# The order of token tiles and weight chunks at the end of five weight products in a two-block transformer kernel

## The chip, the core and the metric

The kernel runs on one core of a Trainium2 chip. The metric is the device time of one execution, in microseconds (us); shorter is better. The kernel before takes 2402.28 us, the median of three runs.

## What is computed

A sequence of 512 tokens of width 1024 passes two blocks in fp32. What matters here are the places where a product with a weight matrix ends a sublayer and a normalisation follows:

```
# first block, twice (MLA layer, then sliding-window layer)
y = attention(x)                       # ends in  o @ w_o          (1024 x 1024)
x = layernorm(alpha * x + y)
x = layernorm(alpha * x + relu(x @ w_up)**2 @ w_down)   # w_down: 4096 x 1024
# second block
y = (gm*(hm @ w_mlstm_out) + gd*(hd @ w_diff_out) + gr*(hr @ w_ret_out)) @ w_out
x = x + rmsnorm(y) ; h2 = rmsnorm(x)
x = x + rmsnorm((silu(a) * u) @ w_ffn_out)
```

## The kernel before

**Products.** Every fp32 factor is split into a high part and a remainder, and a product is three matmuls (high by high, high by remainder, remainder by high; `mm3`, line 590), all written at line 588. Weights come in chunks of 128 x 2048 numbers. Chunk c goes through slot c mod 2: SP loads it into `RAW` (`load`, line 429), ACT copies it to the high part `WH` in two halves (`split`, line 1438), DVE subtracts to get the remainder `WL` in two halves (`split`, line 2102) and then raises `lo_ready`, on which PE waits before it uses the chunk. Since there are two slots, ACT may not write `WH` of chunk c before PE has finished chunk c-2; PE says that with `chunk_done`:

```
if c >= 2:
    act.wait_ge(chunk_done, c - 1 + i * per)                          # line 1447
for part in (slice(0, n // 2), slice(n // 2, n)):
    nc.scalar.activation(WH[s][:, part], RAW[s][:, part], ACT.Copy).then_inc(hi_ready, 1)
```

**A projection by tokens.** The 512 tokens are four tiles of 128, with a PSUM bank `A[t]` each. An output half of 512 columns needs two chunks (kh = 0 and 1), each with four of the eight 128-row pieces of the contraction. So a (tile, chunk) pair is a block of 4 x 3 = 12 matmuls of 512 columns. `tokens` (line 596) takes all four tiles through one chunk, then through the next.

**The last two chunks.** `tokens_edge` (line 627) handles the second output half. It runs over eight blocks in an order written out by hand, waits for the second chunk's `lo_ready` at the first block that uses it, and, ahead of its last block, puts the transposes of the normalised tiles 0 and 1 (`edge_turn`, line 647). `features_edge` (line 659) follows with the first product of the next sublayer, and takes the transposes of tiles 2 and 3 in its middle. `tokens_edge` is called five times: after `w_o` of the MLA layer (line 939, called ln0 below), after the first MLP's `w_down` (line 992, ln1), after `w_o` of the window layer (line 1127, ln2), after the second MLP's `w_down` (line 992, pre), and after `w_out` (line 1395, post). The final `w_ffn_out` product has an order of its own (line 1418) that is not touched. If the first chunk of such an edge is called e, the second is e+1, and it shares its slot with e-1, the last chunk of the first output half.

**Beside it.** While PE takes the first output half, DVE adds the residual and takes half moments of each tile (`residual`, line 466, h = 0; `mlp`, lines 2528 to 2543; `product_out`, line 2865, with ACT's `product_squares`, line 2009, at post), and its `split` of chunk e+1 stands behind the fourth tile of that work. In the second half DVE and ACT normalise each tile as it is finished (`norm_edge`, lines 2448 and 1626; lines 1752 to 1768 for pre; lines 2875 to 2892 and 2028 to 2041 for post). ACT's `split` of the next sublayer's first chunk stands behind the normalisation of tiles 0 and 1 and waits for chunk e to be done, which is when tile 3's block of chunk e ends. POOL only loads vectors here; SP's next load waits for `lo_ready` of e+1.

Of the kernel before, what the change touches and what calls it, by code (L numbers as in the profile page):

```python
# [139 lines left out]
def build(nc, a, out):  # L140
# [53 lines left out]
    def grid(t, k, n, at=0):  # L194
        return t[:, at:at + k * n].rearrange("p (k n) -> p k n", k=k)
# [4 lines left out]
    def tok(t):  # L200
        return slice(t * P, (t + 1) * P)
# [63 lines left out]
    def slot(c):  # L265
        return c % 2
# [319 lines left out]
    def _(pe):  # L586
# [3 lines left out]
        def mm3(dst, lh, ll, rh, rl, first, last):  # L590

            mm(dst, lh, rh, first, False)
            mm(dst, lh, rl, False, False)
            return mm(dst, ll, rh, False, last)
# [32 lines left out]
        def tokens_edge(c, rnd, xh, xl, name, done):  # L627

            pe.wait_ge(lo_ready, c + 1)
            for t, kh in ((0, 0), (1, 0), (0, 1), (1, 1), (2, 0), (3, 0), (2, 1), (3, 1)):  # L630
                wh, wl = grid(WH[slot(c + kh)], 4, 512), grid(WL[slot(c + kh)], 4, 512)
                if kh == 0:
                    pe.wait_ge(a_free[t], rnd)
                elif t == 0:
                    pe.wait_ge(lo_ready, c + 2)
                elif t == 3:
                    for x in range(2):
                        edge_turn(name, x, done)
                for j in range(4):
                    k = 4 * kh + j  # L640
                    m = mm3(A[t][:], xh[:, k, tok(t)], xl[:, k, tok(t)], wh[:, j, :], wl[:, j, :], k == 0, k == KD - 1)
                if t == 3:
                    m.then_inc(chunk_done, 1)
                elif kh:
                    m.then_inc(tok_done, 1)

        def edge_turn(name, t, done):

            half = t // 2
            pe.wait_ge(*done(t))  # L650
            for k in range(KD):
                bank, free, n = edge_bank(name, half, k // 2)
                if t % 2 == 0 and k % 2 == 0:
                    pe.wait_ge(free, n)
                r = nc.tensor.transpose(bank[:, 256 * (k % 2) + P * (t % 2):256 * (k % 2) + P * (t % 2) + P], Y[:, t, tok(k)], ident[:])  # L655
                if t % 2 and k % 2:
                    r.then_inc(turned, 1)
# [279 lines left out]

        tokens(BASE["wo0"][0] + 1, slot(BASE["wo0"][0] + 1), XH, XL, 4, 4, 512, BASE["wo0"][1])
        tokens_edge(BASE["wo0"][0] + 2, BASE["wo0"][1] + 1, XH, XL, "ln0", normed("ln0"))

        def seven(g, name, i):
# [28 lines left out]
        def mlp(name, first, first_done, last, last_done):  # L970

            c0, ra, rb, _, _, _ = BASE[name]
            c3 = c0 + 33

            def down(i, h):
                for kh in range(2):
                    j = 4 + 2 * h + kh
                    pe.wait_ge(mlp_lo, plain_tile(name, 0) + 4 * kh + 4)
                    tokens(c3 + j, slot(c3 + j), YH, YL, 4 * kh, 4, 512, ra + h, kh == 0, kh == 1)

            def up(i, js):
                for j in js:
                    features(c0 + 11 * i + j, slot(c0 + 11 * i + j), XH, XL, rb // 2 + 4 * i + j)

            features_edge(c0, rb // 2, first, first_done)
            for i in range(3):
                up(i, range(0 if i else 1, 4))
                seven((0 if name == "mlp0" else 3) + i, name, i)
            up(3, range(4))
            pe.wait_ge(common_done, SUMMED.index(name) + 1)  # L990
            down(3, 0)
            tokens_edge(c3 + 6, ra + 1, YH, YL, last, last_done)
# [129 lines left out]
        for k in (6, 7):  # L1122
            for t in range(T):
                r = output_products(A[t], t, (k,), False, k == 7)
                if k == 7:
                    r.then_inc(chunk_done if t == T - 1 else tok_done, 1)
        tokens_edge(BASE["wo1"][0] + 2, BASE["wo1"][1] + 1, YH, YL, "ln2", normed("ln2"))
        pre_done = lambda t: (s_("pre_n"), t + 1)
        mlp("mlp1", "ln2", normed("ln2"), "pre", pre_done)
# [1977 lines left out]
```

## Time and profile before

| | |
|---|---|
| median of three runs | 2402.28 us (2401.63 to 2402.39) |
| the profiled execution, its own time | 2400.7 us |
| its span, first to last instruction | 2398.9 us |
| PE busy | 2372.0 us (99%) |
| DVE busy | 1381.7 us (58%) |
| ACT busy | 963.4 us (40%) |
| granted TensorE clock, mean | 1.000 |

PE is TensorE; DVE, ACT, POOL and SP are VectorE, ScalarE, GpSimd and SyncE. A matmul's row shows 0.39 us although the next one starts 0.23 us after it: matmuls overlap, so starts are to be compared, not durations. "idle before" in square brackets is the idle time of the engine before an instruction, with the one that ended it.

### The profile page before, as it was taken

How to read it: one execution, taken by the hardware profiler on the slowest of the kernel's cores; microseconds unless marked ns; L12 is line 12 of the kernel's file. 1: busy time of each engine (PE TensorE's matmuls, PEld its weight loads, DVE VectorE, ACT ScalarE, POOL GpSimd, SP SyncE). 2: the span in 40 equal slices, each digit the busy share in tenths (PEclk: the TensorE clock that was granted, in tenths of full speed). 3: DMA queues.
4: the chain of work that ended last, by engine and by line, in shares of the span. 5: the costliest groups of instructions: out<-in, count | busy, mean ns of one | idle time of the engine just before them, and what ended most of it. 6: DMA issues, size and time to landing. Idle time of an engine off the chain costs nothing.

```text
span 2398.9 us, 29398 instructions
## 1 busy us (share of the span) xinstructions
PE 2372.0 (99%) x11532; PEld 1960.0 (82%) x11532; DVE 1381.7 (58%) x2079; ACT 963.4 (40%) x1720; POOL 72.7 (3%) x146
## 2 busy tenths in 40 slices
PE   8999999999999999999999999999999999999998
PEld 8778888888888888878888888888877888888887
DVE  4667877766668787675544222323356535565655
ACT  4434443335545344344444323323245534433333
POOL 3000000000000000000000000100000000000000
PEclk9999999999999999999999999999999999999999
DMA  4123324333113332322222332222321122323231
GB/s 142 53 74 128 125 81 141 106 106 102 57 54 98 114 104 74 121 88 88 80 78 71 105 105 71 85 73 88 110 64 52 61 89 82 112 70 123 88 123 70
DMA packets 177061, 219.19 MB, mean 91 GB/s; under 512 B 9987, under 2 KB 131040, under 8 KB 176816
## 3 DMA queue, kind: packets, MB, share of 16 engines
q1 hardware_dynamic: 173152, 204.82, 26.5%
q0 software_dynamic: 3792, 12.75, 1.7%
q8 instruction: 81, 1.33, 0.2%
q14 instruction: 36, 0.29, 0.0%
HBM read 215.43 MB, written 5.27 MB: 92 GB/s over the span
## 4 chain that ended last, share of the span: by engine, by line
PE 95%; DVE 3%; ACT 1%; issue 1%; DMA 0%; SPq 0%; DVEq 0%; ACTq 0%
PE B L588 44%; PE A L588 41%; PE C L588 7%; PE C L1045 1%; DVE ar L2318 0%; PE C L1316 0%; DVE WL L2110 0%; DMA X<-in_x 0%; PE C L1154 0%; PE C L655 0%; PE C L874 0%; DVE st L2420 0%; DVE XL L2265 0%; DVE Y L2439 0%; DVE X L2908 0%
## 5 line engine op out<-in xcount | busy, mean ns | idle before, releaser
L2110 DVE TENSOR_TENSOR WL<-RAW,WH 128x1024 fp32r<-128x1024 f32 (+3 forms) x346 | 395.6, 1185 | 383.1 <-ACT WH L1450 382.8
L588 PE MATMUL B<-XH,WH 128*128 128x512 f32 (+1 forms) x1432 | 542.6, 383 | 1.4 <-ACT XH L1507 0.8
L588 PE MATMUL B<-XH,WL 128*128 128x512 f32 (+1 forms) x1432 | 534.9, 377 | 0.0
L588 PE MATMUL B<-XL,WH 128*128 128x512 f32 (+1 forms) x1432 | 519.7, 378 | 2.5 <-DVE XL L2265 2.3
L1450 ACT ACTIVATE WH<-RAW 128x1024 fp32r<-128x1024 f32 (+4 forms) x362 | 353.0, 1026 | 406.9 <-PE A L588 267.1
L588 PEld LDWEIGHTS B<-XH,WH 128*128 128x128 f32 x1432 | 269.2, 188 | 68.1 <-issue 14.1
L588 PEld LDWEIGHTS B<-XH,WL 128*128 128x128 f32 x1432 | 269.2, 188 | 50.5
L588 PEld LDWEIGHTS B<-XL,WH 128*128 128x128 f32 x1432 | 259.7, 188 | 52.1 <-DVE XL L2265 4.1
L588 PE MATMUL A<-WH,XH 128*128 128x512 f32 (+2 forms) x688 | 260.6, 379 | 1.0 <-issue 1.0
L588 PE MATMUL A<-WH,XL 128*128 128x512 f32 (+2 forms) x688 | 259.2, 377 | 0.0
L588 PE MATMUL A<-WL,XH 128*128 128x512 f32 (+2 forms) x688 | 259.1, 377 | 0.0
L588 PE MATMUL A<-WH,YH 128*128 128x512 f32 x608 | 237.7, 391 | 0.2 <-DVE WL L2110 0.2
L588 PE MATMUL A<-WH,YL 128*128 128x512 f32 x608 | 236.8, 389 | 0.0
L588 PE MATMUL A<-WL,YH 128*128 128x512 f32 x608 | 236.7, 389 | 0.0
L588 PEld LDWEIGHTS A<-WH,XH 128*128 128x128 f32 x688 | 129.5, 188 | 25.2 <-issue 2.2
L588 PEld LDWEIGHTS A<-WH,XL 128*128 128x128 f32 x688 | 129.4, 188 | 23.2
L588 PEld LDWEIGHTS A<-WL,XH 128*128 128x128 f32 x688 | 129.5, 188 | 22.8
L588 PEld LDWEIGHTS A<-WH,YH 128*128 128x128 f32 x608 | 114.1, 188 | 24.9 <-DVE WL L2110 0.7
L588 PEld LDWEIGHTS A<-WH,YL 128*128 128x128 f32 x608 | 114.1, 188 | 24.0
L588 PEld LDWEIGHTS A<-WL,YH 128*128 128x128 f32 x608 | 114.2, 188 | 23.1
L588 PE MATMUL A<-ar 64*128 64x256 f32 (+7 forms) x512 | 113.0, 439 | 1.8 <-ACT ar L1839 1.8
L1453 ACT ACTIVATE YH<-ar 128x512 fp32r<-128x512 f32 (+1 forms) x86 | 51.6, 627 | 134.2 <-DVE ar L2129 81.4
(369 smaller groups left out, 2988.9 us busy)
## 6 DMA issues: line engine op xcount, KB each, us to landing
RAW<-in_w_in SPq DMA_DIRECT2D x33, 1024.0 KB, 5.1
RAW<-in_mlp_w_up SPq DMA_DIRECT2D x32, 1024.0 KB, 5.3
RAW<-in_mlp_w_down SPq DMA_DIRECT2D x26, 1024.0 KB, 5.2
RAW<-in_w_in SPq DMA_DIRECT2D x48, 512.0 KB, 4.5
RAW<-in_w_ffn_in SPq DMA_DIRECT2D x22, 1024.0 KB, 5.0
RAW<-in_w_ffn_out SPq DMA_DIRECT2D x8, 1024.0 KB, 5.0
ar<-in_mlp_w_down SPq DMA_DIRECT2D x6, 1024.0 KB, 7.6
RAW<-in_mla_w_o SPq DMA_DIRECT2D x4, 1024.0 KB, 5.0
```

What stands on the lines that cost most here:

```text
L588: return nc.tensor.matmul(dst, l, r, start=first, stop=last)
L1045: r = nc.tensor.transpose(C[kb][:, tok(x)], W_S[:, z, h, blk * P:blk * P + P], ident[:])
L1450: nc.scalar.activation(WH[s][:, part], RAW[s][:, part], ACT.Copy).then_inc(hi_ready, 1)
L1453: return nc.scalar.activation(dst, src, ACT.Copy, scale=scale)
L2110: x = tt(WL[s][:, part], RAW[s][:, part], f32(WH[s][:, part]), ALU.subtract)
```

## The change

One line: the order of the first four blocks in `tokens_edge`. Block (t, kh) is tile t with chunk kh.

```diff
         def tokens_edge(c, rnd, xh, xl, name, done):
 
             pe.wait_ge(lo_ready, c + 1)
-            for t, kh in ((0, 0), (1, 0), (0, 1), (1, 1), (2, 0), (3, 0), (2, 1), (3, 1)):
+            for t, kh in ((0, 0), (0, 1), (1, 0), (1, 1), (2, 0), (3, 0), (2, 1), (3, 1)):
                 wh, wl = grid(WH[slot(c + kh)], 4, 512), grid(WL[slot(c + kh)], 4, 512)
                 if kh == 0:
                     pe.wait_ge(a_free[t], rnd)
                 elif t == 0:
                     pe.wait_ge(lo_ready, c + 2)
```

Tile 0 gets both chunks ahead of tile 1. The matmuls, their number and their operands stay. The wait for the second chunk's `lo_ready` stays with block (0, 1) and so stands after one block of the edge in place of two. Tiles 2 and 3 keep their order.

## Rows read from the trace of the kernel before

**Rows 1.** The page: busy us (share of the span) and count of instructions by engine.
```profile
PE 2372.0 (99%) x11532; PEld 1960.0 (82%) x11532; DVE 1381.7 (58%) x2079; ACT 963.4 (40%) x1720; POOL 72.7 (3%) x146
```

**Rows 2.** PE's waits: line, releaser, us in total, times, longest us.
```profile
PE B L588 <- DVE XL L2265: 2.3, 4, 1.7
PE C L655 <- ACT Y L1453: 1.9, 2, 1.3
...
PE A L588 <- DVE WL L2110: 0.2, 1, 0.2
```

**Rows 3.** Timeline of edge ln0: start us, us, engine, line, what.
```profile
187.29 0.39 PE L588 MATMUL A<-WH,XH 128*128 128x512 f32 x1
...
187.55 2.01 ACT L1450 ACTIVATE WH<-RAW 128x1024 fp32r<-128x1024 f32 x2 [9.92 <-PE A L588]
...
188.83 2.34 DVE L2110 TENSOR_TENSOR WL<-RAW,WH 128x1024 fp32r<-128x1024 f32 x2
...
206.34 0.60 PE L655 MATMUL C<-ident,Y 128*128 128x128 f32 x4
```

**Rows 4.** Timeline of edge ln2, around PE's wait for the second chunk.
```profile
702.25 0.67 DVE L2478 TENSOR_TENSOR Y<-X,A 128x512 f32<-128x512 f32 x1
...
702.75 0.39 PE L588 MATMUL A<-WH,YH 128*128 128x512 f32 x1
...
706.19 2.34 DVE L2110 TENSOR_TENSOR WL<-RAW,WH 128x1024 fp32r<-128x1024 f32 x2
...
707.97 0.39 PE L588 MATMUL A<-WH,YL 128*128 128x512 f32 x1
708.59 0.50 PE L588 MATMUL A<-WH,YH 128*128 128x512 f32 x1 [0.23 <-DVE WL L2110]
...
709.15 0.39 PE L588 MATMUL A<-WH,YL 128*128 128x512 f32 x1
```

**Rows 5.** Timeline of edge ln1: first matmul and DVE's split.
```profile
526.43 0.39 PE L588 MATMUL A<-WH,YH 128*128 128x512 f32 x1
...
527.97 2.34 DVE L2110 TENSOR_TENSOR WL<-RAW,WH 128x1024 fp32r<-128x1024 f32 x2
```

**Rows 6.** Timeline of edge pre: first matmul and DVE's split.
```profile
1042.77 0.39 PE L588 MATMUL A<-WH,YH 128*128 128x512 f32 x1
...
1044.31 2.35 DVE L2110 TENSOR_TENSOR WL<-RAW,WH 128x1024 fp32r<-128x1024 f32 x2
```

**Rows 7.** Timeline of edge post: first matmul and DVE's split.
```profile
2015.64 0.39 PE L588 MATMUL A<-WH,XH 128*128 128x512 f32 x1
...
2017.51 2.36 DVE L2110 TENSOR_TENSOR WL<-RAW,WH 128x1024 fp32r<-128x1024 f32 x2 [0.20 <-ACT WH L1450]
```

**Rows 8.** Timeline of edge ln0: the normalised tile 1, and the next chunk's split.
```profile
201.95 1.15 ACT L1453 ACTIVATE Y<-Y,st 128x1024 f32<-128x1024 f32 x1 [1.23 <-DVE st L2441]
203.87 2.01 ACT L1450 ACTIVATE WH<-RAW 128x1024 fp32r<-128x1024 f32 x2 [0.77 <-PE A L588]
```

**Rows 9.** Timeline of edge pre: ACT and PE ahead of tile 1's transposes.
```profile
1059.35 2.01 ACT L1450 ACTIVATE WH<-RAW 128x1024 fp32r<-128x1024 f32 x2 [0.75 <-PE A L588]
...
1064.16 0.66 PE L655 MATMUL C<-ident,Y 128*128 128x128 f32 x4 [1.30 <-ACT Y L1453]
```

**Rows 10.** Timeline of edge post: ACT's chain after tile 1, and PE's wait on it.
```profile
2027.44 0.29 ACT L2020 ACTIVATE st<-st 128x1 f32<-128x1 f32 x1
2027.84 1.06 ACT L1738 ACTIVATE Y<-X 128x1024 f32<-128x1024 f32 x1
...
2046.51 0.66 PE L655 MATMUL C<-ident,Y 128*128 128x128 f32 x4 [0.57 <-ACT Y L1453]
```

**Rows 11.** Windows: us; busy PE, PEld, DVE, ACT, POOL; granted clock; DMA share, GB/s.
```profile
1072.00:1076.00 4.00, 2.51 (x19) 2.29 (x20) 3.80 (x10) 3.48 (x6) 0.00 (x0) 1.00 0.00 0
```

**Rows 12.** Timeline of PE at the kernel's start, transposes after a long idle stretch.
```profile
4.93 1.09 PE L729 MATMUL A<-ident,X 128*128 128x128 f32 x4 [4.93 <-DMA X<-in_x]
...
12.04 1.06 PE L729 MATMUL A<-ident,X 128*128 128x128 f32 x4
```

## The prediction

> **What bounds the kernel now.** I read the page first: PE is busy for 2372.0 us, 99% of the span of 2398.9 [rows 1]. So a microsecond in which PE stands still is a microsecond of the kernel, unless a later wait of PE shrinks by as much; and work of DVE or ACT is worth something only where PE waits for it. The second view is therefore PE's list of waits [rows 2]: what a faster normalisation could give back at the five edges is small, 1.9 us in two waits for a normalised tile ahead of its transposes and 2.3 us in four waits for remainders. One line of that list is on the very spot of the change: once, for 0.2 us, PE waited for a weight remainder (WL) in front of a token product. The third view is the timeline of each of the five edges, for two questions: when does the second chunk become ready, and when does PE ask for it, before and after.
>
> **The step of PE.** In edge ln0 the first matmul starts at 187.29 and the first transpose, behind seven blocks or 84 matmuls, at 206.34 [rows 3]: 19.05 / 84 = 0.227 us for a matmul, 2.72 us for a block of 12. In the order of before, PE asks for the second chunk two blocks (5.44 us) after the edge's start. The change makes it ask after one block, at 2.72 us.
>
> **When the second chunk is ready.** It shares its slot with the chunk that PE finishes at the edge's start, so ACT cannot begin its copy earlier: it begins at 187.55, 0.26 us after the edge's first matmul, and needs 2.01 us for both halves; DVE's subtraction stands behind its work on tile 3's first half and runs from 188.83 for 2.34 us, to 191.17 [rows 3]. That is 3.88 us after the edge's start: earlier than 5.44, later than 2.72. Nothing of this moves with the change, as all of it stands ahead of the first moved instruction. So a wait that was hidden behind the second block comes into the open.
>
> **What a wait costs.** Edge ln2 has this wait already [rows 4]: DVE's remainder ends at 706.19 + 2.34 = 708.53 and PE's matmul starts at 708.59, 0.06 later. The third matmul from there starts at 709.15, where an unbroken stream would have had it at 707.97 + 3 x 0.227 = 708.65, so the stream slipped by 0.50 us, of which 708.59 - 708.20 = 0.39 is waiting and 0.10 to 0.11 is slow restart. (The 0.23 in brackets is less because the previous matmul's own row lasts 0.39.) So I take for each edge: slip = end of WL + 0.06 + 0.10 - (edge start + 2.72).
>
> - ln0 [rows 3]: 191.17 + 0.16 - 190.01 = 1.32 us.
> - ln1 [rows 5]: WL ends 530.31; 530.47 - 529.15 = 1.32 us.
> - ln2 [rows 4]: WL ends 708.53; 708.69 - 705.47 = 3.22, less the 0.50 that it costs already: 2.72 us, just one block. Here the first half's product comes from a special order, all four tiles end close together, and DVE has their four residuals and half moments queued ahead of its subtraction (the second residual, at 702.25, is shown).
> - pre [rows 6]: WL ends 1046.66; 1046.82 - 1045.49 = 1.33 us.
> - post [rows 7]: WL ends 2019.87; 2020.03 - 2018.36 = 1.67 us. ACT squares tile 3 before its copy, which makes this later than the others.
>
> Sum of the slips: 1.32 + 1.32 + 2.72 + 1.33 + 1.67 = 8.36 us.
>
> **What is queued behind the wait.** On PE everything: tile 1's first block had covered it. Tile 0 is nevertheless finished earlier, by 2.72 less the gross slip (1.4 us in ln0, ln1 and pre, 1.05 in post, nothing in ln2, where it ends when it did); tile 1 and all after it are later by the full slip. The wait for tile 1's free bank costs nothing: even in ln2, where DVE is latest, it frees that bank at 702.25 + 0.67 = 702.92 [rows 4], and PE now asks for it after 708.59. SP's next load waits for `lo_ready` of the same chunk, which does not move; POOL waits only for normalised tiles and has nothing urgent.
>
> **Does the earlier tile 0 give something back?** What PE needs from it is the normalised tiles 0 and 1 in front of block (3, 1). In ln0 tile 1 is ready at 201.95 + 1.15 = 203.10 and PE comes to its transposes at 206.34 [rows 3, 8]: 3.2 us of slack, and both ends get later together. What follows on ACT and DVE hangs on the end of block (3, 0), for which ACT's next copy waits at 203.87 [rows 8]; that moves with PE. ln1 and ln2 look the same. Gain: nothing. In pre PE does wait, 1.30 us ahead of tile 1's transposes, but the chain behind it starts at ACT's copy of the next chunk at 1059.35, which waited 0.75 us for PE's block (3, 0); the squares, root and scaling of tile 1 stand behind that copy in ACT's order, and the scaling is what released PE at 1064.16 [rows 9]. This chain moves with PE, so the 1.30 stays, and so does the longest wait for remainders (1.7 us of rows 2), whose DVE chain starts from the same copy. Gain: 0, bounded by the 1.30. In post ACT has no such anchor: from the arrival of tile 1 it runs nearly unbroken to the wait of 0.57 at 2046.51. There the earlier tile 0 takes away a small gap: the root of tile 1 starts at 2027.44 and lasts 0.29, and the squares of tile 0, which wait for DVE's sum, start at 2027.84 [rows 10]. The gap is 0.11 by the rows' ends and 0.40 by their starts; ACT's rows overlap a little, so I take 0.20. Gain 0.20, bounded by the wait of 0.57. Together: 8.36 - 0.20 = 8.2 us.
>
> **The clock.** The new stall in ln2 is about 3.1 us of no matmul starts (705.47 to 708.59), the longest in the body of the kernel; the longest of before there is the 1.7 of rows 2, and the window that holds it shows a granted clock of 1.00, the 2.4 GHz level [rows 11]. So no row shows what 3 us do. The only longer idle is at the kernel's start: after 4.93 us without one, four transposes' rows last 1.09 us, and 1.06 still at 12.04 [rows 12], against 0.60 for four of the same shape in an edge [rows 3]. So that stretch ran at about half speed, for 12.04 + 1.06 - 4.93 = 8.2 us. A stretch at half speed costs half its length, so the price here is between 0 and 4.1 us. I take 0, since the stall is nearer to the 1.7 us one, which left the clock alone, and is a single one with dense matmuls on both sides. The Trainium skill, TensorE: Matmul & The Clock Gate, Part 1, says that an idle array falls to 1.2 GHz and gets 2.4 GHz back only after sustained work; that is the case just priced. The same page (Loop structure matters more than you think) would finish one output tile over the whole contraction before the next, which is what the change does for tile 0; its reason is a warm clock, and here the clock is at 1.00 either way [rows 11], so by that rule the sum gets no gain.
>
> **Rivals.**
> - *Half clock behind ln2's stall.* As above; a gain in nothing, a further cost of up to 4.1 us, around 1.6 if the stretch is as long as the stall: 2412.0 us, at most 2414.5. For it: 3.1 us is nearer to 4.93 than any stall before in the body. Against: the body's rows at 1.00. Chance 0.10.
> - *The slips are partly given back.* The waits of pre and post (1.30, 1.7, 0.57) shrink because DVE and ACT had 1 to 3 us more for tile 0: 8.4 - 3.6 = 4.8 us, 2407.1 us, at the border of no change. For it: these engines set the waits. Against: in pre the chain is anchored at PE's own block (3, 0). Chance 0.06.
> - *Faster: tile 0 first shortens the path to the transposes.* The place is the wait ahead of tile 1's transposes and the remainders behind it. If the second chunk were ready when PE asks, there would be no slips, and up to 1.9 + 2.3 = 4.2 us of waits [rows 2] would go: 2398.1 us. It decides where WL ends before edge start + 2.72 us; it ends 3.88, 3.88, 5.78, 3.89 and 4.23 us after the start in the five edges, later in all. Chance 0.02.
>
> **How the numbers follow.** The forecast (all five slips, nearly nothing back) has 0.82. The sum is made against the profiled execution, 2400.7 us with a span of 2398.9, so 2408.9; the median of the runs is 1.6 above that execution, and the same 8.2 us on 2402.28 give 2410.4. Range: below, both bounds of giveback (1.3 and 0.4 more) and the 1.6 between executions: 2407.1; above, the half clock at most of its bound, 2414.0. Some 0.2%, 4.8 us, is what a measurement of this kernel can tell from no change; 8.2 is 0.34%. Slower by more takes the forecast, the clock rival and a part of the second: 0.93; within it 0.05; faster 0.02.
>
> **What the profile after would show.** PE waiting for WL five times in place of once, with bracketed idle of about 1.05, 1.05, 2.95, 1.05 and 1.4 us (each slip less 0.10 and less the 0.16 by which a matmul's row overhangs), 7.5 in total; WL's end unmoved against the edge's start; first transposes of ln0 at 207.66, and the edges' slips adding up to 1.3, 2.6, 5.4, 6.7, 8.2; the wait of 1.30 in pre still there and the one of 0.57 in post near 0.3; the granted clock at 1.00 behind 708 + 3. I am wrong if WL ends earlier in an edge, if the pre wait shrinks, or if matmuls behind ln2's stall start 0.43 us apart.

## The result

The changed kernel takes 2410.22 us (median of seven executions, 2408.99 to 2411.35) beside 2402.24 us for the kernel before (seven, 2400.67 to 2402.64): 8.0 us more, ratio 1.0037 with a 95% interval of 1.0028 to 1.0046. It is slower, by about what the five waits add up to. The profiled execution took 2408.99 us, its span is 2407.2.

The profile after is best opened at PE's waits (line, releaser, us in total, times, longest us):

```profile
PE A L588 <- DVE WL L2110: 7.5, 5, 3.0
PE A L729 <- DMA X<-in_x: 6.5, 2, 5.1
PE B L588 <- DVE XL L2265: 2.3, 4, 1.7
...
PE C L655 <- ACT Y L1453: 1.6, 2, 1.3
```

One line has moved to the top: the wait for the second chunk's remainder was 0.2 us, once [rows 2], and is 7.5 us in five. The two kinds of wait that an earlier tile 0 might have shortened are at 2.3 and 1.6 us, where they were 2.3 and 1.9.

The five places, and with each the first transpose of that edge, from the timeline (start us, us, engine, line, what):

```profile
186.03 0.39 PE L588 MATMUL A<-WH,XH 128*128 128x512 f32 x1
187.56 2.34 DVE L2110 TENSOR_TENSOR WL<-RAW,WH 128x1024 fp32r<-128x1024 f32 x2
189.96 0.50 PE L588 MATMUL A<-WH,XH 128*128 128x512 f32 x1 [1.05 <-DVE WL L2110]
206.41 0.60 PE L655 MATMUL C<-ident,Y 128*128 128x128 f32 x4
...
526.85 0.39 PE L588 MATMUL A<-WH,YH 128*128 128x512 f32 x1
530.77 0.50 PE L588 MATMUL A<-WH,YH 128*128 128x512 f32 x1 [1.05 <-DVE WL L2110]
547.23 0.60 PE L655 MATMUL C<-ident,Y 128*128 128x128 f32 x4
...
704.40 0.39 PE L588 MATMUL A<-WH,YH 128*128 128x512 f32 x1
707.84 2.34 DVE L2110 TENSOR_TENSOR WL<-RAW,WH 128x1024 fp32r<-128x1024 f32 x2
710.23 0.50 PE L588 MATMUL A<-WH,YH 128*128 128x512 f32 x1 [2.95 <-DVE WL L2110]
726.69 0.60 PE L655 MATMUL C<-ident,Y 128*128 128x128 f32 x4
...
1046.86 0.39 PE L588 MATMUL A<-WH,YH 128*128 128x512 f32 x1
1050.79 0.50 PE L588 MATMUL A<-WH,YH 128*128 128x512 f32 x1 [1.05 <-DVE WL L2110]
1067.25 0.60 PE L655 MATMUL C<-ident,Y 128*128 128x128 f32 x4
1069.59 0.66 PE L655 MATMUL C<-ident,Y 128*128 128x128 f32 x4 [1.30 <-ACT Y L1453]
...
2022.45 0.39 PE L588 MATMUL A<-WH,XH 128*128 128x512 f32 x1
2026.74 0.50 PE L588 MATMUL A<-WH,XH 128*128 128x512 f32 x1 [1.40 <-DVE WL L2110]
2043.22 0.60 PE L655 MATMUL C<-ident,Y 128*128 128x128 f32 x4
...
2054.81 0.66 PE L655 MATMUL C<-ident,Y 128*128 128x128 f32 x4 [0.34 <-ACT Y L1453]
```

The first row of each group is the edge's first matmul. From it to the first transpose PE needs 20.38, 20.38, 22.29, 20.39 and 20.77 us. Before it was 19.05 in ln0 [rows 3], 19.58 in ln2 (702.75 [rows 4] to 722.33) and 19.05 or 19.04 in the others. So the slips are 1.33, 1.33, 2.71, 1.34 and 1.73 us, 8.44 in all; and from the first transpose of post to that of tile 3 the time went from 11.83 us to 11.59, which gives 0.24 back. DVE's remainder ends 187.56 + 2.34 - 186.03 = 3.87 us after the start of ln0, where it ended at 3.88 [rows 3], and at 5.78 in ln2 as before [rows 4].

The two profiled spans differ by 2407.2 - 2398.9 = 8.3 us, and that is 8.44 - 0.24 = 8.20 plus two things that nearly cancel and belong to no edge's order. This execution reached its first edge 187.29 - 186.03 = 1.26 us earlier, most of which it had at its first matrix product already (12.82 against 13.97 us). And behind the transposes of edge pre, the clock fell for a while (windows: us; busy PE, PEld, DVE, ACT, POOL; granted clock; DMA share; GB/s):

```profile
1078.00:1080.00 2.00, 1.07 (x6) 0.87 (x7) 1.80 (x7) 1.75 (x4) 0.00 (x0) 1.00 0.00 0
1080.00:1082.00 2.00, 2.00 (x14) 2.00 (x13) 2.00 (x5) 1.15 (x1) 0.00 (x0) 0.66 0.00 0
1082.00:1084.00 2.00, 2.00 (x12) 2.00 (x11) 1.81 (x2) 0.03 (x1) 0.00 (x0) 0.50 0.00 0
1084.00:1086.00 2.00, 1.85 (x13) 1.42 (x12) 1.15 (x3) 2.00 (x6) 0.00 (x0) 0.99 0.42 75
```

0.50 is the 1.2 GHz level. PE had just stood for 1.66 us, up to 1078.89, waiting for a remainder of the activations. From the first transpose of pre to the first matmul of its second half it took 1084.87 - 1067.25 = 17.62 us, against 1078.06 - 1061.82 = 16.24 before: 1.38 us, the price of this fall.

A caution on the mean clock of a whole execution, which is all that the executions without a profile have. In every one of the twelve profiles the granted clock falls to 0.50 once more, in the last microseconds, where PE has nothing left to do and the fall costs nothing. The kernel with the old order and the chunk by halves (below) has a mean of 0.999 by this alone; while PE works, no window of its profile is below 1.00 (its last full microsecond):

```profile
2395.00:2396.00 1.00, 0.00 (x0) 0.00 (x0) 0.00 (x0) 0.00 (x0) 0.00 (x0) 0.50 1.04 385
```

So a mean of 0.999 does not say that a fall cost anything; the changed kernel's profile, with its 1.38 us, has 0.999 too. Of the twelve profiles only the two with a fall of over 2 us behind ln2 have 0.998.

### The profile page after: what moved, and what is told of

It is laid out like the page before. It is cut to its first block, busy times and chain, and to the rows that moved or that the text cites. A ratio compares the mean times of both kernels' runs of the same rounds, so it can differ in the third digit from the quotient of the medians.

```text
span 2407.2 us, 29398 instructions
## 1 busy us (share of the span) xinstructions
PE 2372.8 (99%) x11532; PEld 1959.2 (81%) x11532; DVE 1381.5 (57%) x2079; ACT 962.8 (40%) x1720; POOL 72.7 (3%) x146
## 3 DMA queue, kind: packets, MB, share of 16 engines
q8 instruction: 81, 1.33, 0.2%
## 4 chain that ended last, share of the span: by engine, by line
PE 94%; DVE 4%; ACT 1%; issue 1%; DMA 0%; SPq 0%; DVEq 0%; ACTq 0%
PE B L588 44%; PE A L588 41%; PE C L588 7%; DVE WL L2110 1%; PE C L1045 1%; DVE ar L2318 0%; PE C L1316 0%; DVE st L2420 0%; DMA X<-in_x 0%; PE C L1154 0%; PE C L655 0%; DVE XL L2265 0%; PE C L874 0%; PE A L655 0%; ACT XH L1453 0%
```

## The experiments

Ten runs follow, of nine new kernels and of the changed one again. Those measured together share one measurement of the kernel before: 2400.77 us (27 executions) for the first four, 2401.10 (28) for the next four, 2401.42 (13) for the last two. Edges are named ln0, ln1, ln2, pre and post as above.

**The wait alone.** The order stays that of before; the wait stands one block earlier.

```diff
                 if kh == 0:
                     pe.wait_ge(a_free[t], rnd)
-                elif t == 0:
-                    pe.wait_ge(lo_ready, c + 2)
+                    if t == 1:
+                        pe.wait_ge(lo_ready, c + 2)
                 elif t == 3:
```

> The order of the blocks is that of the kernel before; only PE's wait for the second chunk stands after one block, as in the changed kernel. Theory (all of the loss is the earlier wait): the same five slips of 1.32, 1.32, 2.72, 1.33 and 1.67 us, 8.4 us in all, 2410.6 us, and PE waiting for WL five times for 7.5 us; the wait of 0.57 in post stays at about 0.5, since tile 0 gains nothing. Rival (the new order costs or gives something of its own, such as another sequence of banks): over 1 us away from the changed kernel.

2411.53 us (2409.67 to 2411.98, five), +10.8, ratio 1.0041 (1.0027 to 1.0055). Five waits for WL, 8.0 us in all; the one in post for tile 3 is 0.56, so that nothing is given back there. The wait alone makes the whole loss and more. The expectation's sign for the rival, over 1 us away from the changed kernel, was met (1.3 us by the medians, 2.8 by the differences to the kernel before), but the profile gives other reasons. Each wait is 0.09 or 0.10 us longer here (1.14 in brackets in place of 1.05), and in ln0 PE starts 0.15 us behind the end of WL in place of 0.06. So the five slips, read as above, are 1.40, 1.42, 2.8, 1.42 and 1.75 us, 8.8 in all; why PE starts later, no run shows. The rest in the profiled execution is the clock, in the very stall where the prediction had looked for it (PE's timeline, and windows as above):

```profile
711.33 0.77 PE L588 MATMUL A<-WH,YH 128*128 128x512 f32 x1 [3.05 <-DVE WL L2110]
711.89 0.63 PE L588 MATMUL A<-WL,YH 128*128 128x512 f32 x1
712.31 0.63 PE L588 MATMUL A<-WH,YL 128*128 128x512 f32 x1
...
730.59 0.60 PE L655 MATMUL C<-ident,Y 128*128 128x128 f32 x4
```

```profile
708.00:712.00 4.00, 0.95 (x4) 0.61 (x3) 3.15 (x4) 0.97 (x1) 0.00 (x0) 0.82 0.00 0
712.00:716.00 4.00, 4.00 (x11) 3.17 (x10) 0.00 (x0) 0.00 (x0) 0.00 (x0) 0.50 0.83 260
716.00:720.00 4.00, 4.00 (x16) 3.19 (x16) 0.10 (x1) 0.00 (x0) 0.00 (x0) 0.83 0.02 6
```

Some 14 matmuls start 0.43 us apart in place of 0.23, 2.8 us lost.

**The new order in ln2 alone.** `tokens_edge` chooses by name; the other four edges keep the order of before.

```diff
-            for t, kh in ((0, 0), (1, 0), (0, 1), (1, 1), ...
+            early = name in ('ln2',)
+            for t, kh in ((0, 0), (0, 1) if early else (1, 0), (1, 0) if early else (0, 1), (1, 1), ...
```

> The new order in edge ln2 alone. Theory (slips are independent and add up): +2.7 us, 2405.0 us, a bracketed wait for WL of 2.95 us, all other edges as before and the clock at 1.00 throughout. Rival (the long stall lowers the clock behind it): matmuls behind 708 us of the trace start 0.43 us apart for a stretch, +4 to +6 us. Second rival (part is taken back later): under +2 us.

2405.11 us (2403.24 to 2408.75, eleven), +4.3, ratio 1.0019 (1.0010 to 1.0028). The profiled execution is the shortest one, +2.5, with the clock at 1.00 throughout and this wait:

```profile
708.67 0.50 PE L588 MATMUL A<-WH,YH 128*128 128x512 f32 x1 [2.96 <-DVE WL L2111]
```

Its ln2 took 725.13 - 702.83 = 22.30 us, 2.72 more than before, as forecast. The median of +4.3 lies at the lower end of the rival's +4 to +6, while the profile is the theory's. The spread of 5.5 us, against 3.0 of the kernel before, suggests that in part of the executions something is added to the 2.7; that it is the clock, no profile of this kernel shows.

**The new order in pre alone.** The same edit with `('pre',)`.

> The new order in edge pre alone, whose profile after the change showed the clock at 0.50 for some 3 us behind three idle stretches (1.05, 1.30 and 1.66 us). Theory A (three idle stretches close together lower the clock, and the new 1.05 us one was what was missing): +1.3 us of slip and +1.4 us of clock, 2405 us, with the clock below 1.00 behind the wait of 1.66 us in the profile and in the mean clock of most runs. Theory B (the fall is a matter of chance in each run and of no single edge): +1.3 us, 2403.6 us, the clock at 1.000 in most runs.

2402.22 us (2400.69 to 2403.15, eleven), +1.45, ratio 1.0004 (0.9995 to 1.0013), which the measurement can't tell from no change; in the profile the slip is there (1.05 in brackets), the waits of 1.30 and 1.66 behind it too, and the clock stays at 1.00. So pre's own three idle stretches do not bring the fall each time: by this profile theory A has fallen, though its +2.7 us is still inside the interval of the times. Theory B's sign, 1.000 in most executions, was not seen: it stands on three of eleven here and on five of the 27 of the kernel before. But 0.999 comes about by the end of the kernel alone, so this sign can tell neither way.

**The new order, chunk taken by halves.** DVE signals the first half of WL (`first` is set for the second chunk of each of the five edges, `edge` counts them), and block (0, 1) needs the second only from its third piece on.

```diff
                 elif t == 0:
-                    pe.wait_ge(lo_ready, c + 2)
+                    pe.wait_ge(s_("lo_first"), edge + 1)
 ...
                 for j in range(4):
                     k = 4 * kh + j
+                    if t == 0 and k == 6:
+                        pe.wait_ge(lo_ready, c + 2)
 ...
                 x = tt(WL[s][:, part], RAW[s][:, part], f32(WH[s][:, part]), ALU.subtract)
+                if first and half == 0:
+                    x.then_inc(s_("lo_first"), 1)
```

> The new order in all five edges, but block (0, 1) starts when the first half of the second chunk's WL is there and waits for the second half only ahead of its third piece of the contraction. Theory (it is the readiness of the chunk that costs, not the order): WL's first half ends 1.17 us before the second, so slips of about 0.15 in ln0, ln1 and pre, 0.5 in post and 1.55 in ln2, less 0.2 given back in post: +2.3 us against the kernel before, 2404.6 us. Rival (the loss comes from the order itself): still +7 us or more.

2403.57 us (2402.96 to 2405.04, eleven), +2.8, ratio 1.0012 (1.0003 to 1.0021). Same order as the changed kernel, and two thirds of the loss are gone. PE's waits:

```profile
PE A L588 <- DVE WL L2113: 2.1, 2, 1.8
...
PE C L658 <- ACT Y L1456: 1.6, 2, 1.3
```

In ln0, ln1 and pre the wait is too short for the list; post has 0.27 and ln2 1.82, a slip of 1.58 (21.16 us from first matmul to first transpose, against 19.58). So it is mainly the readiness of the chunk that costs, and what is left is again mostly a wait for it, in ln2.

**The order of before, chunk by halves.** The same edit on the kernel before.

> The order of the kernel before, with the second chunk taken by halves: block (0, 1) starts on the first half of WL. It takes away the one wait that the kernel before has, in ln2 (0.23 us in brackets, 0.50 us of slip). Theory (readiness sets the slip): -0.5 us, 2400.3 us beside 2400.8, no line of PE waiting for WL. Rival (halves cost something of their own, a semaphore more in each edge): no change or slower.

2400.24 us (2398.84 to 2402.18, eleven), 0.9 less, ratio 0.9997 (0.9988 to 1.0006). PE no longer waits for WL anywhere, and ln2 takes 720.64 - 701.59 = 19.05 us, 0.53 less than before. The profile shows the gain; the times alone don't resolve it. It is the lowest median here, but not by more than the times can resolve.

**The order of before, WL ahead of tile 3 in ln2.**

```diff
-                if h or n % 2:
+                if (h and n == 0) or n % 2:
                     split(c0 + 2 * h + 1)
 ...
                 for t in range(T):
+                    if n == 2 and h == 0 and t == 3:
+                        split(c0 + 3)
                     wait_tok(dve, t, g0 + h, c0 + 2 * h + 1)
```

> The order of the kernel before; in ln2 DVE makes the second chunk's WL ahead of the residual of tile 3 and its half moments. Theory (DVE's queue is what makes WL late in ln2): WL ends 1.3 us earlier against the edge's start, the 0.23 us wait is gone, -0.5 us. Rival (tile 3's bank, freed 2.3 us later, becomes the wait): a wait for DVE Y in front of block (3, 0), no gain.

2400.64 us (2399.67 to 2402.08, eleven), 0.5 less, ratio 0.9998 (0.9989 to 1.0007): again below what the times can show, but ln2 takes 721.48 - 702.44 = 19.04 us and the wait is gone. On DVE the subtraction now stands between the residuals:

```profile
703.95 0.70 DVE L2420 BATCH_NORM_STATS2 st<-Y 128x6 f32<-128x512 f32 x1
704.57 2.34 DVE L2110 TENSOR_TENSOR WL<-RAW,WH 128x1024 fp32r<-128x1024 f32 x2
706.82 0.68 DVE L2480 TENSOR_TENSOR Y<-X,A 128x512 f32<-128x512 f32 x1
```

It ends at 706.91, 4.47 us after the edge's start in place of 5.78, and no wait for bank 3 has appeared. DVE's queue is what makes ln2 the worst of the five.

**Ln2 alone, with twice the subtraction.** On the new order in ln2 only, DVE writes WL of the second chunk an extra time ahead of its `split`.

```diff
+                if h and n == 2:
+                    w = slot(c0 + 3)
+                    for half in range(2):
+                        dve.wait_ge(hi_ready, 2 * (c0 + 3) + half + 1)
+                        part = slice(1024 * half, 1024 * half + 1024)
+                        then(tt(WL[w][:, part], RAW[w][:, part], f32(WH[w][:, part]), ALU.subtract))
                 if h or n % 2:
                     split(c0 + 2 * h + 1)
```

> The new order in ln2 alone, and DVE subtracts WL of the second chunk twice there, so that the wait grows by some 2.4 us to about 5.4 in brackets. Theory (a wait at this place adds its whole length, and the clock falls behind a stall of this length always, where behind 3 us it falls in part of the runs): slip of 5.1 us and 2.8 us of clock, +7.9 us, 2408.7 us, with a small spread, and in the profile matmuls 0.43 us apart behind it. Rival (the fall in the wait-only kernel was chance and has nothing to do with the stall's length): +5.1 us in at least half of the runs, clock at 1.000.

2408.82 us (2406.86 to 2409.69, six), +7.7, ratio 1.0031 (1.0019 to 1.0043), with 0.998 as the mean clock of all six executions.

```profile
711.39 0.80 PE L588 MATMUL A<-WH,YH 128*128 128x512 f32 x1 [5.47 <-DVE WL L2111]
...
730.37 0.60 PE L656 MATMUL C<-ident,Y 128*128 128x128 f32 x4
```

```profile
712.00:716.00 4.00, 4.00 (x11) 3.14 (x10) 0.00 (x0) 0.00 (x0) 0.00 (x0) 0.50 0.79 260
716.00:720.00 4.00, 4.00 (x18) 3.25 (x17) 2.94 (x5) 0.29 (x1) 0.00 (x0) 0.90 0.02 7
```

The edge took 730.37 - 703.04 = 27.33 us, 7.75 more than in the kernel before: 5.2 of slip (the bracket grew from 0.23 to 5.47) and 2.5 of clock.

**Ln2 alone, with WL ahead of tile 3.** Both edits, on the order that is new in ln2 only.

> The new order in ln2 alone, and WL made ahead of tile 3's residual there, so that the stall shrinks from 2.95 to about 1.6 us in brackets. Theory: slip of 1.4 us against the kernel before and the clock not falling at this place, so +1.4 us, 2402.2 us, without the runs of +5 and more that the new order in ln2 alone had. Rival (the large runs come from elsewhere): median still 1.5 us above slip, +2.9 us.

2402.43 us (2400.75 to 2403.86, eleven), +1.3, ratio 1.0005 (0.9996 to 1.0014). Its wait:

```profile
707.74 0.50 PE L588 MATMUL A<-WH,YH 128*128 128x512 f32 x1 [1.64 <-DVE WL L2111]
```

The edge took 724.20 - 703.22 = 20.98 us, 1.40 more than before. With a stall of 1.6 us the median is the slip and nothing besides; with 3.0 us it was 1.6 above the slip. The two intervals reach from -1.0 to +3.4 us and from +2.4 to +6.7, so that this difference of 1.6 is a hint and not shown.

**The changed kernel again, and with WL ahead of tile 3 in ln2.** Both were measured together.

> The changed kernel once more, on the chip of the next run. The wait-only kernel came out 10.8 us above the kernel before where the changed kernel stood 8.0 above it, measured apart. Theory (both have the same stalls, and the clock falls behind ln2's 3 us in part of the executions of either): +8 to +11 us, executions spread over 2 us and more, those with a lower mean clock being the longer. Rival (the new order is itself worth some 2 us against the wait alone): +8.0 or less, little spread.

2410.14 us (2409.20 to 2411.10, five), +8.7, ratio 1.0038 (1.0025 to 1.0052). The spread is 1.9 us, not over 2, and all five executions show a mean clock of 0.999, so the expectation that the longer ones have the lower clock was not borne out. The waits are those of the first profile to the hundredth, and the fall of the clock is again in pre and not in ln2.

> The changed kernel, with WL of the second chunk made ahead of tile 3's residual in ln2, so that this stall is 1.6 us in brackets in place of 2.95. Theory: 1.3 us less slip, and besides it the clock no longer falls behind ln2, so 1.3 to 3 us below the changed kernel on the same chip; four other waits unchanged (1.05, 1.05, 1.05, 1.40). Rival (clock falls follow no stall): 1.3 us below it at most.

2407.77 us (2406.80 to 2408.95, nine), ratio to before 1.0027 (1.0017 to 1.0037), 2.4 below the changed kernel beside it, of which 1.3 is slip by the waits (2.95 became 1.64, the four others stayed). The remaining 1.1 points the way of the theory, but is half the spread of one kernel's executions. And in the two profiles, whose spans differ by 2.4 us as well, it has another place: behind ln2 the clock is at 1.00 in both, and the fall of 1.4 us is in edge pre, in the changed kernel only, though the waits there are the same (windows of the changed kernel, then of this one):

```profile
1040.00:1095.00 55.00, 50.68 (x271) 43.16 (x270) 39.68 (x64) 25.95 (x46) 0.00 (x0) 0.97 0.25 77
...
1040.00:1095.00 55.00, 50.67 (x277) 42.83 (x276) 40.85 (x63) 28.45 (x48) 0.00 (x0) 1.00 0.24 76
```

So this pair does not show that a shorter stall in ln2 saves clock in ln2.

## Why the prediction was right

The forecast was 2410.4 us, 8.2 above the kernel before; measured 2410.22 and 8.0 (8.7 in the second set).

- *The step of PE and the end of WL.* PE asks for the second chunk after 2.72 us in place of 5.44, and WL ends where it ended: right, to 0.01 us in ln0 and ln2.
- *The price of a wait*, taken from the one wait that the kernel before had: slips of 1.32, 1.32, 2.72, 1.33 and 1.67 were forecast, 1.33, 1.33, 2.71, 1.34 and 1.73 measured. This is what carried the forecast: the change's own stall stood in the trace of before once, with its restart. The bracketed waits of 1.05, 1.05, 2.95, 1.05 and 1.40 came out exactly. Only the absolute time of ln0's transposes, 206.41 and not 207.66, is off, by the 1.26 us of the kernel's start.
- *That the wait is the cause and not the order* is shown from both sides: the wait alone costs it all (+10.8 with the clock's part), and the new order with the chunk taken sooner costs 2.8, two thirds less, of which 1.58 is the slip that ln2 keeps.
- *What comes back.* Nothing in ln0, ln1 and ln2; the 1.30 in pre stayed, since its chain starts at ACT's copy behind PE's own block (3, 0); post gave 0.24 where 0.20 was said. The wait-only kernel, in which tile 0 is not finished earlier, keeps its 0.56 in post, so that it is the earlier tile that gave the 0.24.
- *Additivity.* Single edges gave their own slips in their profiles: 2.72 for ln2, and 1063.77 - 1043.38 - 19.05 = 1.34 for pre.
- *The clock.* Here the reasoning was incomplete. It said 0 for the changed kernel and gave a fall behind ln2's stall a chance of 0.10. In both profiled executions of the changed kernel the clock behind ln2 was at 1.00, as forecast. But it fell behind a stall of 3.05 us, 0.1 longer, in the wait-only kernel (2.8 us), behind 5.47 us in the one profile of it (2.5 us), and in the changed kernel's two profiles in pre, by 1.4 us, behind a wait of 1.66 that in the profile of before had left it alone. The argument "nearer to the 1.7 us stall" treated it as settled by length, from one execution. So the term was put at nothing, and the profile of the changed kernel shows 1.38 there. That its span still met the forecast within 0.1 us (2407.2 beside 2398.9 + 8.2) is luck: the kernel's start was 1.26 us shorter. How much clock the medians hold, before and after, the mean clock cannot tell: the kernel before has executions at 0.998 too (16 of 68), longer than its others by 1.5, 0.9 and 0.2 us in the three sets, and none of them has a profile. The slips of 8.2 us are the part of the forecast that the profiles bear out. By the Trainium skill, TensorE: Matmul & The Clock Gate, Part 1, the array falls to 1.2 GHz when it idles; the windows of the doubled kernel agree (0.50 behind 5.47 us of idle), and those behind 3 us agree only at times. What decides at 3 us these runs leave open: the three profiles without a fall have 2.95 or 2.96 in brackets, the one with it 3.05, so that chance and the 0.1 us are not told apart. Why the clock falls in pre in the changed kernel is open as well.
- *The bound on such a fall.* The 4.1 us from the kernel's start were high; 1.4, 2.5 and 2.8 us were seen. The 8.2 us that were halved for it were not all work at half speed: they hold a wait of PE of 1.71 us for the input (the row at 9.85, below), without which the same working gives 3.2 us.

## What to carry to other kernels

Before blocks are reordered so that one result is finished sooner, find for each input the time at which it is ready, and compare it with the new time of asking: a wait that is hidden behind one block of other work costs its full remainder once that block goes. Here each second chunk was ready 3.9 to 5.8 us after an edge's start and PE now asked at 2.7, in exchange for an earlier tile for which PE waited in one place only, where it gave 0.24 us. Where a consumer needs only the first half of a chunk at first, signalling by halves took two thirds of the loss away; with the order of before it was 0.9 us ahead, which the times do not resolve.

## What the runs showed of the hardware

A stall does not cost the same in each kernel and execution. In the profiles, behind 1.64 us nothing was added in ln2 (two profiles), behind 2.95 or 2.96 us nothing (three), behind 3.05 us 2.8 us by half clock (one), and behind 5.47 us 2.5 us (one, and a mean clock of 0.998 in all six executions). In pre, the same three waits of 1.05, 1.30 and 1.66 us were followed by a fall in two profiles and by none in two others. The half-speed stretch was about 14 matmuls of 512 columns in the wait-only kernel, 0.43 us apart.

The start of the kernel varies likewise: four transposes of the same kind took 1.12 us at 9.85 in the profile of before and 0.66 us at 9.68 after, though no instruction there differs; the granted clock of both windows reads 1.00, so there the spacing of the rows tells more than that column (the profile of before, then of after).

```profile
9.85 1.12 PE L729 MATMUL A<-ident,X 128*128 128x128 f32 x4 [1.71 <-DMA X<-in_x]
...
9.68 0.66 PE L729 MATMUL A<-ident,X 128*128 128x128 f32 x4 [1.35 <-DMA X<-in_x]
```
